# Two transformer blocks on one core: the end of the FFT convolution taken one token tile at a time, and two vector steps moved at the boundary behind it

## The reference

```python
def conformer_conv(h, w_pw1, b_pw1, w_dw, b_dw, ln_g, ln_b, w_pw2, b_pw2):
    u = h @ w_pw1 + b_pw1
    a, g = jnp.split(u, 2, axis=-1)
    u = a * jax.nn.sigmoid(g)
    u = depthwise_conv(u, w_dw) + b_dw          # 31 taps over the tokens
    u = jax.nn.silu(layer_norm(u, ln_g, ln_b))
    return u @ w_pw2 + b_pw2

x = x + rms_norm(m, g[1])                        # m: what conformer_conv returned
h = rms_norm(x, g[2])                            # input of the MLP
```

## Time and profile before

| | |
|---|---|
| median of three runs | 902.14 us |
| profiled execution, its own time | 899.98 us |
| its span | 898.2 us |
| PE busy share of the span | 98% |
| DVE, ACT, POOL | 77%, 32%, 33% |
| granted TensorE clock, mean | 0.997 |
| stretch of the change | about 338 to 400 us of the span |

### The profile page before, as it was taken

One profiled execution on the slowest core, in us unless ns is written; L12 is line 12 of the kernel. 1 busy time (PEld: TensorE's weight loads), 2 busy tenths in 40 slices (PEclk: granted clock), 3 DMA queues, 4 the chain that ended last, 5 costly groups with the idle time before them and its releaser, 6 DMA issues.

```text
span 898.2 us, 12926 instructions
## 1 busy us (share of the span) xinstructions
PE 883.8 (98%) x4851; PEld 743.1 (83%) x4851; DVE 691.8 (77%) x731; ACT 289.5 (32%) x567; POOL 297.8 (33%) x205
## 2 busy tenths in 40 slices
PE   9999999999999999999999999999999999999997
PEld 7987798888887787788888888888767988888885
DVE  6699888777777775889777778778578887776775
ACT  6648271111112501354111111554676541111112
POOL 2230223444434432213444443331152223333331
PEclk9999999999999999999999999999999999999999
DMA  8960627555558265216655555366043376555541
GB/s 283 337 231 1 234 98 234 190 191 196 193 223 289 82 202 188 93 68 232 219 192 194 192 204 169 124 236 219 16 189 96 102 239 221 187 186 188 187 163 47
DMA packets 82263, 160.23 MB, mean 178 GB/s; under 512 B 5080, under 2 KB 40426, under 8 KB 82224
## 3 DMA queue, kind: packets, MB, share of 16 engines
q1 hardware_dynamic: 82208, 159.69, 51.8%
q10 hardware_dynamic: 16, 0.00, 0.0%
HBM read 158.63 MB, written 1.05 MB: 178 GB/s over the span
## 4 chain that ended last, share of the span: by engine, by line
PE 88%; DMA 4%; ACT 3%; DVE 2%; POOL 1%; issue 1%; SPq 0%; DVEq 0%; POOLq 0%; ACTq 0%
PE ps L2165 84%; PE ps L2169 3%; DMA raw<-in_even_w_in 2%; DMA raw<-in_odd_w_pw 2%; ACT arena L1665 1%; ACT arena L2057 1%; POOL w_hi L636 0%; DVE arena L1499 0%; ACT arena L1853 0%; DVE w_lo L864 0%; POOL st L675 0%; POOL st L751 0%; DVE x_res L957 0%; DVE st L1495 0%; POOL st L674 0%
## 5 line engine op out<-in xcount | busy, mean ns | idle before, releaser
L864 DVE TENSOR_TENSOR w_lo<-raw,w_hi 128x2048 fp32r<-128x2048 f32 (+2 forms) x134 | 308.9, 2328 | 38.9 <-POOL w_hi L845 21.8
L2165 PE MATMUL ps<-act_hl,w_hi 128*128 128x512 f32 (+1 forms) x1088 | 241.2, 367 | 0.6 <-POOL w_hi L658 0.2
L2165 PEld LDWEIGHTS ps<-act_hl,w_hi 128*128 128x128 f32 x1088 | 182.4, 189 | 30.0 <-issue 1.0
L2165 PE MATMUL ps<-w_hi,act_hl 128*128 128x512 f32 (+3 forms) x656 | 180.9, 382 | 1.2 <-DVE w_lo L864 0.8
L2165 PE MATMUL ps<-w_hi,hl 128*128 128x512 f32 (+1 forms) x648 | 178.3, 388 | 0.0
L651 POOL TENSOR_SCALAR w_hi<-raw 128x2048 fp32r<-128x2048 f32 x48 | 119.0, 2480 | 149.6 <-PE ps L2165 138.7
L2165 PEld LDWEIGHTS ps<-w_hi,act_hl 128*128 128x128 f32 x656 | 118.6, 188 | 25.2 <-issue 3.5
L2165 PEld LDWEIGHTS ps<-w_hi,hl 128*128 128x128 f32 x648 | 119.2, 188 | 23.3
L2165 PEld LDWEIGHTS ps<-act_hl,w_lo 128*128 128x128 f32 x960 | 129.2, 191 | 8.2
L2165 PE MATMUL ps<-act_hl,w_lo 128*128 128x256 f32 x960 | 132.3, 282 | 0.0
L636 POOL TENSOR_SCALAR w_hi<-raw 128x2048 fp32r<-128x2048 f32 (+2 forms) x22 | 50.0, 2276 | 163.9 <-PE ps L2165 111.2
(11 more groups left out here) (241 smaller groups left out, 825.4 us busy)
## 6 DMA issues: line engine op xcount, KB each, us to landing
raw<-in_mlp_w SPq DMA_DIRECT2D x64, 1024.0 KB, 5.2
raw<-in_w_gate SPq DMA_DIRECT2D x22, 512.0 KB, 3.9
raw<-in_w_up SPq DMA_DIRECT2D x22, 512.0 KB, 4.9
raw<-in_w_down SPq DMA_DIRECT2D x11, 1024.0 KB, 5.0
raw<-in_odd_w_pw SPq DMA_DIRECT2D x16, 512.0 KB, 6.2
raw<-in_w_in SPq DMA_DIRECT2D x8, 1024.0 KB, 6.1
raw<-in_even_w_in SPq DMA_DIRECT2D x4, 1024.0 KB, 12.3
raw<-in_even_w_out SPq DMA_DIRECT2D x4, 1024.0 KB, 5.7
```

The lines of the kernel that those rows point to most:

```text
L864: tt(w_lo[slot_of(n)][:, 0:w], raw[slot_of(n)][:, 0:w], w_hi[slot_of(n)][:, 0:w].bitcast(F32), ALU.subtract).then_inc(S("w_split"), pieces ...
L2165: return pe.matmul(o, l, r, start=start, stop=stop, skip_group_check=True)
```

## The change

- `zz` has four buffers, one for each block, and `filtered` no longer waits for an older inverse.
- `inverse(b)` does only tile 0's part: `direct(b, 0)` and the two middle products of tile 0. After `inverse(3)`, a loop over the four blocks does tile 1's parts.
- `keep_warm` is gone from the turn. The turn goes by tile and half: `turn_z(m, j)` transposes four k of one tile; groups, gain and bias, silu, high and low parts are by tile too.
- On DVE tile 0 is normed first, and tile 1's statistics and shift come between steps of tile 0. ACT norms all of tile 1.
- `pw2` goes by piece and tile, with the transposes of tile 1 between the products of tile 0. The two last steps, by halves of tile 1, stay, but over pieces 1 to 3 of which piece 0 is done before.
- `gains_product(1, 5)` waits for `ln_shift` and not for the last silu; its result and `pre_1` lie elsewhere.
- At this boundary `post_gain(0)` stands ahead of `lo_until(last + 1)`.

```diff
-        zz = [AR(1536 * i, 2, BLOCKS, T) for i in range(2)]
+        zz = [AR(at, 2, BLOCKS, T) for at in (0, 1536, 4608, 6144)]
...
-        Z_GROUPS = ((0, 1), (1, 1), (2, 2), (4, 2), (6, 2))
+        Z_GROUPS = ((0, 0, 2), (0, 2, 2), (1, 0, 2), (0, 4, 4), (1, 2, 2), (1, 4, 4))
...
-                gp.wait_ge(S("silu"), len(Z_GROUPS))
+                gp.wait_ge(S("ln_shift"), 1)
                 gains_product(1, 5)
...
-                    pre_tile_1(g + 1)
-                    lo_until(last + 1)
-                    post_gain(0)
+                    pre_tile_1(at, g + 1)
+                    if s == 3:
+                        post_gain(0)
+                        lo_until(last + 1)
+                    else:
+                        lo_until(last + 1)
+                        post_gain(0)
...
-                            if b >= 2:
-                                dve.wait_ge(S("inv"), 2 * (b - 2) + 2)
...
+                row_stats(0, 1)
+                moments(0)
                 row_stats(1, 0)
...
                 dve.wait_ge(S("ln_rstd"), 1)
-                layer_norm(0, 0, 512).then_inc(S("normed"), 1)
+                layer_norm(0, 0)
+                layer_norm(0, 1)
+                z_odd(0, 1)
+                z_odd(0, 3)
+                silu(0)
+                row_stats(1, 1)
+                z_low(0)
+                moments(1)
+                silu(1)
+                z_low(1)
+                z_odd(0, 5)
+                z_odd(0, 7)
                 dve.wait_ge(S("ln_rstd"), 2)
                 tsc(ln_shift, mv[:, 1, 0:1], rstd[:, 1:2], -1.0, ALU.mult, ALU.mult).then_inc(S("ln_shift"), 1)
...
+                z_even(0, 0)
+                z_tanh(0)
+                z_even(0, 2)
+                z_high(0)
+                z_tanh(1)
+                z_high(1)
+                z_even(0, 4)
+                z_even(0, 6)
                 act.wait_ge(S("ln_shift"), 1)
...
+                def turn_z(m, j):
+
+                    if m == 0:
+                        normed[0] += 1
+                        pe.wait_ge(S("normed"), normed[0])
+                    else:
+                        pe.wait_ge(S("normed_1"), j + 1)
+                        pe.wait_ge(S("z"), 2 * j + 2)
+                        pe.wait_ge(S("z_odd"), 2 * j + 2)
+                    for k in range(4 * j, 4 * j + 4):
+                        ins = turn(z_bank(m, k), nrm[:, m, k * P:(k + 1) * P])
+                    ins.then_inc(S("z_turned"), 1)
...
+                def middle(b, m):
+
+                    q, at, half = b // 2, T * (b % 2), (slice(64, P), slice(0, 64))[m]
+                    for j in range(2):
+                        ins = mm(ps[half, ACC + 2 * m + q, at:at + T], inv_t[:, 2 * MIDDLE + j, half], zz[b][:, j, MIDDLE, :],
+                                 False, True)
+                    return ins
...
                     pe.wait_ge(S("zz"), 2 * b + 1)
-                    direct(0)
+                    direct(b, 0)
                     pe.wait_ge(S("zz"), 2 * b + 2)
...
-                    direct(1).then_inc(S("inv"), 1)
+                    ins = middle(b, 0)
+                    if b % 2:
+                        ins.then_inc(S("inv"), 1)
...
                 inverse(3)
-                turn_normed()
...
+                for b in range(4):
+                    direct(b, 1)
+                    ins = middle(b, 1)
+                    if b % 2:
+                        ins.then_inc(S("inv"), 1)
+                turn_z(0, 0)
+                turn_z(0, 1)
+                pw2_bias(0)
...
+                need_lows(lows[0] + 1)
+                pw2(0, 0)
+                turn_z(1, 0)
+                need_lows(lows[0] + 2)
+                pw2(1, 0)
+                turn_z(1, 1)
+                pw2_bias(1)
+                need_lows(lows[0] + 3)
+                pw2(0, 1, free=True)
+                need_lows(lows[0] + 4)
+                pw2(2, 0)
+                pw2(3, 0).then_inc(S("tile_out"), 1)
+                for h in range(2):
+                    for j in range(1, 4):
+                        need_lows(lows[0] + (5 if j == 1 else 6))
+                        if h and j == 3:
+                            turn_m(TURN_BANK[3], 0)
+                        ins = pw2(j, 1, half=h, free=h == 1)
```

More of the change, by code:

```diff
@@ L944, in add_pre_half @@
                     dve.wait_ge(S("gained_1"), 2 * SCALE_LATER.index(s) + h + 1)
-                    stt(nrm[:, 1, half[h]], nrm[:, 1, half[h]], rs_post[:, 1:2], pre_1[:, half[h]], ALU.mult, ALU.add)\
+                    stt(nrm[:, 1, half[h]], nrm[:, 1, half[h]], rs_post[:, 1:2], pre_1[SCALE_LATER.index(s)][:, half[h]],
+                        ALU.mult, ALU.add)\
                         .then_inc(S("normed"), 1)
@@ L1350, in _, with moments @@
                 row_stats(0, 0)
-                row_stats(1, 0)
[L1352 to L1358, removed]
-                dve.wait_ge(S("ln_rstd"), 1)
-                layer_norm(0, 0, 512).then_inc(S("normed"), 1)
+                def moments(m):
+                    dve.bn_aggr(mv[:, m, :], bns[:, m, :, :]).then_inc(S("ln_stats"), 1)
@@ new lines, in layer_norm, with z_odd @@
+                def layer_norm(m, h):
+                    c = slice(512 * h, 512 * h + 512)
+                    tsc(nrm[:, m, c], tall_out(ACC, m)[:, c], mv[:, m, 0:1], rstd[:, m:m + 1], ALU.subtract, ALU.mult)\
+                        .then_inc(S("normed"), 1)
+                def z_odd(m, k):
+                    dve.wait_ge(S("z_turned"), 2 * m + k // 4 + 1)
+                    tsc(zb[:, k, m * P:(m + 1) * P], z_bank(m, k), vcol("ln_g", k), vcol("ln_b", k), ALU.mult, ALU.add)\
+                        .then_inc(S("z_odd"), 1)
@@ L1379, in z_low @@
[L1379 to L1391, removed]
+                z_odd(1, 1)
+                z_odd(1, 3)
                 silu(2)
-                z_low(1)
@@ L1400, in _ @@
                 z_low(4)
+                z_odd(1, 5)
+                z_odd(1, 7)
+                silu(5)
+                z_low(5)
                 lo_until(FIRST["pw2"] + 3)
@@ L1946, in _, with z_even, z_tanh @@
                         f(u_mid[half, :], nrm[half, m, T * b:T * b + T], ACT.Copy).then_inc(S("u_mid"), 1)
+                def z_even(m, k):
+                    act.wait_ge(S("z_turned"), 2 * m + k // 4 + 1)
+                    f(zb[:, k, m * P:(m + 1) * P], z_bank(m, k), ACT.Identity, bias=vcol("ln_b", k), scale=vcol("ln_g", k))\
+                        .then_inc(S("z"), 1)
+                def z_tanh(g):
+                    act.wait_ge(S("z"), z_sum(g))
+                    act.wait_ge(S("z_odd"), z_sum(g))
+                    f(z_part(eb, g), z_part(zb, g), ACT.Tanh, scale=0.5).then_inc(S("z_tanh"), 1)
@@ L1948, in _, with z_high @@
+                def z_high(g):
+                    act.wait_ge(S("silu"), g + 1)
+                    f(z_part(act_hl[:, :, 0:T], g), z_part(zb, g), ACT.Copy, scale=0.5).then_inc(S("act_hi"), 1)
+                z_even(0, 0)
[6 more added lines that the diff above has]
+                z_even(0, 6)
                 act.wait_ge(S("ln_shift"), 1)
-                for h in (slice(0, 512), slice(512, 768)):
+                for h in (slice(0, 512), slice(512, D)):
@@ L1966, in z_high @@
[L1966 to L1976, removed]
+                z_even(1, 0)
                 z_tanh(2)
-                z_high(1)
-                z_even(4)
+                z_even(1, 2)
                 z_high(2)
                 z_tanh(3)
-                z_even(6)
```

107 lines of the change are left out of this document (43 added, 64 removed).

## The result

The changed kernel took 904.23 us (median of 20 runs, 902.68 to 907.11), beside 900.68 us (20 runs, 899.53 to 904.65) for the kernel before on the same chip: ratio 1.0035, interval 1.0026 to 1.0043, so by the ratio 3.2 us slower (2.3 to 3.9); the two medians by themselves lie 3.5 us apart. It was forecast as 3.2 us slower, and that this would be under the bound of 0.5%. It is, but with 20 runs of each it can be told from none. The kernel before came out at 900.68 here where its first three runs had given 902.14, and the absolute time moved with it.

What follows compares the result with a forecast made beforehand. PE, busy 98% of the span, was taken as the bound. Inverse transforms +4.8, keep_warm -3.0, old waits -0.8, new waits and restarts +2.2 gave +3.2 us: median 902.14 to 905.3 us, 8-in-10 range 901.0 to 908.5.

Steps and rivals of the forecast that it cites:

- Inverse transforms: First term: breaking the half-array pairs makes a block take 4.14 us, not 2.94; +4.8 us for four blocks.
- upper bound of 5.2: Highest cost in us given for the inverse transforms, with every step at 0.24 us.
- `keep_warm` and the old waits: Removable between the last inverse transform and pw2: 3.0 us of filler products and 0.8 us of waiting, -3.8 us.
- The layer norm: Tile 0's norm at the turn: hidden behind the put-off loop with 1.7 us to spare.
- A loop of 5.9 us: Put-off loop as with pairs, instead of 8.3 us; the layer norm would still be just in time.
- The first new wait: PE stands still before pw2 for the first low parts: 1.9 us, bounds 1.1 and 3.0.
- The second new wait: After pw2(0, 0), turn_z(1, 0) waits 0.2 us for ACT's norm of tile 1.
- The boundary: From pw2 to the MLP: x and nrm just hidden with 0.3 us of room; taken as 0.
- rival 2: At the boundary, pre_1 beside POOL's rounding takes 2.93 us: +1.5, in all +4.7, 906.8 us; chance 0.13.
- Rival 1: In the inverse transforms, lone half products are cheap: first term 0, sum -1.6 us, 900.5 us; chance 0.12.
- rival 3: Granted clock falls to half in the new wait: +1.7 us, in all +4.9, 907.0 us; chance 0.11.
- rival 4: Faster by over 0.5%: removing all 3.8 us at no cost gives 898.3 us, not over the bound; no separate chance.

Runs made afterwards that it cites:

- e1: Kernel before, with the full-array direct(1) put between tile 0's and tile 1's half-array products in each inverse transform; 905.25 us, ratio 1.0047 to the kernel before.
- e8: Kernel before, with both upper half-array products of a block first, then both lower, nothing between; one execution, 901.13 us.
- e2: Kernel before, with only the turn's fourteen keep_warm products taken out; 901.98 us, ratio 1.0008 to the kernel before.
- e4: Changed kernel, with each block's four half-array products kept together in inverse(b) and only direct(b, 1) put off; 900.2 us, ratio 0.9993 to the kernel before.
- e7: Changed kernel, with the split of the MLP's first weight piece moved ahead of the turn's last low part; 903.16 us, ratio 1.0027 to the kernel before.
- e3: Changed kernel, with the split of the MLP's first weight piece back ahead of post_gain(0); 904.67 us, ratio 1.0032 to the kernel before.

## Why the prediction was right, point by point

**Inverse transforms.** Predicted +4.8, found +4.62 in after and +4.60 in e1, which has nothing else in it. Per put-off block 4.14 / 2 = 2.07 was predicted and 2.05 found; the loop was to take 8.3 and to end at 368.8, and it took 8.2 and ended at 368.7 (369.95 less the lag of 1.2). The mechanism, overlap of the halves and nothing cheaper in a lone one, holds (e1). The picture of neighbours was too narrow, without effect on the sum (e8). The upper bound of 5.2 does not follow from its own step: sixteen steps of 0.24 are 3.86 us for a block and 3.7 more for four, less than what was found; 5.2 comes out if the 0.20 of the change of form, already inside the 0.24, is counted again.

**`keep_warm` and the old waits.** Predicted -3.8. Together with what follows this is right: from the end of the inverse products to `pw2` it was 6.65 us and is 3.29. But the credit needs a condition that I did not write down. The ten and four products stood over waits and held the clock; taken out alone they give back nothing, the stage even loses 0.78 (e2). The 3.0 us are a gain in the changed kernel only because put-off work covers the norm. The first term is not the price of this cover: e4 puts off full-array products alone, and has the cover for 0.4 us (3.68 from the end of the inverse products to `pw2`, beside 3.29).

**The layer norm.** PE comes to it with no wait in after, as predicted. A loop of 5.9 us "would still be just in time", I wrote. e4 has a shorter loop still, since the middle products are not in it, and there PE waits 0.33.

**The first new wait.** Predicted 1.9, at 370.3 to 372.15; found 1.80, from 371.34 to 373.14, less the lag 370.1 to 371.9. PE's own work in it was to be 1.4 and is 1.39. The chain from the first transpose to the first product of `pw2` was to be 3.35 and is 3.19. Its terms hold: the narrow gain and bias that tanh waits for takes 0.46 on ACT (0.45), and two on DVE take 0.73 side by side with it:

```profile
370.64 0.73 DVE L1379 TENSOR_SCALAR arena<-ps,col 128x128 f32<-128x128 f32 x2 [2.46 <-PE ps L2196]
...
371.94 0.69 DVE L1353 BATCH_NORM_STATS2 st<-ps 128x6 f32<-128x512 f32 x1
372.66 0.42 DVE L1392 SCALAR_TENSOR_TENSOR act_hl<-arena,act_hl 128x256 fp32r<-128x256 f32 x1
```

```profile
370.64 0.46 ACT L1975 ACTIVATE arena<-ps,col 128x128 f32<-128x128 f32 x1 [14.91 <-PE ps L2196]
```

The 0.16 that the chain is shorter lie in the hand-offs: ACT and DVE start 0.69 us after the first transpose and not 0.80, and the low part is followed by PE's product within 0.06. The statistics stand between silu and low part with their full 0.69, as predicted.

**The second new wait** was to be 0.2, ended by ACT's norm. It is not there:

```profile
375.20 1.45 ACT L1999 ACTIVATE nrm<-ps,st 128x512 f32<-128x512 f32 x2 [0.56 <-DVE st L1412]
```

Both halves take 1.45 us together; the first is over just when PE is there at 376.03.

**The boundary.** Here I had 0, with 0.3 us of room, and "if PE waits in `turn_m`" stood among the signs that the forecast is wrong. It waits, and it costs 0.70 us (e7). By my own sign this part of the forecast failed. The point of decision was rightly placed, `nrm`'s second half later than 394.7, and it came at 396.16, 394.9 without the lag. The price of rival 2 (1.5) and its cause are not what happened: `pre_1` ran in 1.28, and POOL rounded its piece under the last silu. I had computed the way from `post_gain(0)` to x over DVE alone and left out POOL's 0.30 us step in between, which has to wait for a split that begins at the same time. That x waits for POOL could be read in the earlier trace rows, at 387.10. In the stage the terms are: +4.62 - 3.02 - 0.8 + 1.80 + 0.70 = +3.3, of 3.55 measured. The 0.25 left are of the size of three gaps where products and transposes change places: 0.10 ahead of the first transpose (30.84 to 30.94), and two products that take 0.55 and not 0.45 at 376.44 and at 379.64.

The Trainium skill's page "SBUF — State Buffer" (SBUF: two separate sides) says that GpSimd and a DVE instruction with two SBUF inputs take a shared port pair in turn. I had cited it and applied it to silu, where it cost nothing that ended a wait. The trace agrees where I did not look: 2.39 us against 0.30. The rule was there, the list of POOL's instructions on the new path was not gone through.

**Sizes as a whole.** Without the 0.70 the stage gives +2.85, with it +3.55, and the time +3.2 (2.3 to 3.9): that the forecast of +3.2 was met so closely is luck, because two errors have opposite signs: 0.7 left out at the boundary, and 0.35 too much in all else (3.2 against 2.85). The direction and the largest term are not luck (e1, e4). Rival 1 is refuted and rival 3 did not occur; of rival 2 the place and the sign were right, the cause and the price not. Nothing was to be gained over 0.5% (rival 4), and the best kernel found gains 0.3%. A slip without effect: PE's wait at the start of the trace before is 1.13 us, so that trace has no wait of 1.9 at all.

## What to carry to other kernels

Before cutting a group of products in two to start something sooner, look whether the cut goes through work that runs at the same time: here products on the two halves of the array, and the cut made half of each of them cost as much as the whole. Put off what fills the array alone, and put it where the next wait will be. When a long vector instruction is moved, follow the chain that it now overlaps through every engine, small steps on GpSimd included; and before filler products are counted as waste, ask what they cover and whether the clock holds without them.

## What the runs showed of the hardware

- Products on the upper and lower half of the array overlap within a contiguous group in both orders tried (1.02 us as upper, upper, lower, lower; 1.01 in alternation), and they start out of the program's order (e8); a full-array product between them ends the overlap (two groups of 1.01).
- A GpSimd step on one column (0.30 us) took 2.39 us when it began 0.06 us after a DVE split of 2.29 us with two inputs from SBUF. The last silu of after took 1.89 us beside POOL's rounding, where silu of the same size takes 0.69 without it:

```profile
379.12 0.69 DVE L1385 SCALAR_TENSOR_TENSOR arena<-arena 128x512 f32<-128x512 f32 x1
...
383.84 1.89 DVE L1385 SCALAR_TENSOR_TENSOR arena<-arena 128x512 f32<-128x512 f32 x1 [0.76 <-ACT arena L1982]
```

```profile
383.27 1.92 POOL L647 TENSOR_SCALAR w_hi<-raw 128x2048 fp32r<-128x2048 f32 x1 [5.63 <-PE ps L2192]
```

- The granted clock fell to half for 3.4 us behind, or at the end of, two waits close together: 1.86 and 0.86 us (e2, at 370.4), 1.09 and 0.99 (e2, at 12), 1.38 and 0.95 (e3, at 12). It stayed at 1.00 behind single waits of 1.63 (after), 1.19 (after, at 49) and 1.13 (e4, at 9.7).
